# Both MLPs of a two-layer decoder step in two phases, with the second layer as seven block products over four groups of K tiles

## What is computed

```python
def squared_relu_mlp(xn, w1, w2):
    return jnp.square(jax.nn.relu(xn @ w1)) @ w2

for layer in range(DEPTH):
    xn = rms_norm(x, norm_mix[layer])
    ...
    x = x + y
    x = x + squared_relu_mlp(rms_norm(x, norm_mlp[layer]), mlp_w1[layer], mlp_w2[layer])
```

## Time and profile before

| | |
|---|---|
| median of three runs | 2669.82 us (2668.07 to 2671.2) |
| span of the profiled execution | 2668.4 us |
| busy: PE, VectorE (DVE), ScalarE (ACT), GpSimd (POOL) | 98%, 64%, 37%, 1% of the span |
| granted TensorE clock | 0.996 of full speed |
| MLP 0, from the first plain unit | 406.6 us to about 1136 us |
| MLP 1 | 1929.7 to 2660 us, then output tiles to the end |

### The profile page before, as it was taken

One profiled execution on the slowest core, in us unless ns is written; L12 is line 12 of the kernel. 1 busy time (PEld: TensorE's weight loads), 2 busy tenths in 40 slices (PEclk: granted clock), 3 DMA queues, 4 the chain that ended last, 5 costly groups with the idle time before them and its releaser, 6 DMA issues.

```text
span 2668.4 us, 48443 instructions
## 1 busy us (share of the span) xinstructions
PE 2628.0 (98%) x19052; PEld 2574.4 (96%) x19052; DVE 1709.1 (64%) x2622; ACT 980.5 (37%) x1555; POOL 24.9 (1%) x48
## 2 busy tenths in 40 slices
PE   8999999999999999999999999989999999999999
PEld 8999999999999999999999899978899999999999
DVE  5444447766666666754345898876686666666675
ACT  3111124323232323355245877755542222222222
POOL 0000000000000000000000100000000000000000
PEclk9999999999999999999999999989999999999999
DMA  3111111111010101125325566443311111111112
GB/s 116 47 47 39 48 49 34 54 34 61 31 63 31 63 31 63 32 82 160 114 76 152 130 162 155 99 147 131 99 42 40 55 39 55 39 55 39 55 39 82
DMA packets 208045, 193.05 MB, mean 72 GB/s; under 512 B 16208, under 2 KB 181008, under 8 KB 207938
## 3 DMA queue, kind: packets, MB, share of 16 engines
q1 hardware_dynamic: 188678, 182.50, 22.9%
q10 hardware_dynamic: 19260, 9.09, 1.2%
HBM read 160.93 MB, written 30.49 MB: 72 GB/s over the span
## 4 chain that ended last, share of the span: by engine, by line
PE 78%; DVE 3%; ACT 2%; issue 1%; ACTq 0%; DMA 0%; DVEq 0%
PE ps L760 29%; PE ps L748 23%; PE ps L533 13%; PE ps L1090 2%; PE ps L1005 1%; PE ps L940 1%; PE ps L1091 1%; PE ps L1092 1%; PE ps L1007 1%; PE ps L1296 1%; PE ps L1138 1%; PE ps L571 1%; PE ps L634 1%; PE ps L1200 0%; PE ps L1201 0%
## 5 line engine op out<-in xcount | busy, mean ns | idle before, releaser
L878 DVE TENSOR_TENSOR acc<-ps,acc 128x536 f32<-128x536 f32 x512 | 366.5, 717 | 254.8 <-PE ps L760 254.2
L760 PE MATMUL ps<-hidden_hi,w_hi 128*128 128x268 f32 x2048 | 423.4, 288 | 3.4 <-DVE hidden_lo L2509 1.7
L760 PE MATMUL ps<-hidden_hi,w_lo 128*128 128x268 f32 x2048 | 422.7, 288 | 0.0
L760 PE MATMUL ps<-hidden_lo,w_hi 128*128 128x268 f32 x2048 | 421.6, 287 | 0.0
L760 PEld LDWEIGHTS ps<-hidden_hi,w_hi 128*128 128x128 f32 x2048 | 321.2, 189 | 4.4 <-DVE hidden_lo L2509 2.1
L760 PEld LDWEIGHTS ps<-hidden_lo,w_hi 128*128 128x128 f32 x2048 | 322.4, 189 | 0.0
L760 PEld LDWEIGHTS ps<-hidden_hi,w_lo 128*128 128x128 f32 x2048 | 320.8, 189 | 0.0
L533 PE MATMUL ps<-x_hi,w_hi 128*128 128x358 f32 x1248 | 277.3, 330 | 4.3 <-DVE w_lo L517 4.3
L533 PE MATMUL ps<-x_hi,w_lo 128*128 128x358 f32 x1248 | 273.8, 327 | 0.0
L533 PE MATMUL ps<-x_lo,w_hi 128*128 128x358 f32 x1248 | 273.3, 327 | 0.0
L517 DVE TENSOR_TENSOR w_lo<-w_raw,w_hi 128x1024 fp32r<-128x1024 f32 x76 | 92.8, 1221 | 257.8 <-ACT w_hi L509 257.8
(11 more groups left out here) (340 smaller groups left out, 5130.9 us busy)
## 6 DMA issues: line engine op xcount, KB each, us to landing
w_raw<-in_mlp_w SPq DMA_DIRECT2D x68, 512.0 KB, 4.1
raw_a<-in_mlp_w SPq DMA_DIRECT2D x120, 256.0 KB, 3.0
w_raw<-in_conv_w_in SPq DMA_DIRECT2D x24, 512.0 KB, 3.7
w_raw<-in_w_kv SPq DMA_DIRECT2D x16, 512.0 KB, 4.9
w_raw<-in_w_o SPq DMA_DIRECT2D x16, 512.0 KB, 4.0
k_page<-in_cache_k SPq DMA_DIRECT2D x16, 512.0 KB, 4.8
v_page<-in_cache_v SPq DMA_DIRECT2D x16, 512.0 KB, 4.8
kh_rows<-staged_hi SPq DMA_DIRECT2D x8, 520.0 KB, 2.7
```

What stands on the lines that cost most here:

```text
L760: mm = pe.matmul(PS[:, 2 * p + g, 0:QW], w[k][:, P * m:P * m + P], x[:, k, a:a + QW], start=(k == 0 and j == 0), stop=(k == 1 and j == 2))
L878: dve.tensor_tensor(x, pair(p), x, ALU.add).then_inc(down_read, 1)
```

## The change

The MLP is cut into two phases.

Phase 1 runs the seven products of the 15 blocks back to back, without the second layer between them. The squares are no longer split; each quarter (128 x 536) is stored to DRAM (`h_rows`) by SyncE's queue (`store_hidden`). VectorE's preparation for the next block, which lay in `downs`, moves into `block`. `UB` becomes three buffers, and `u_sum` waits for the stores. The hidden tiles of the two plain units stay in SBUF.

Phase 2 first does the plain units' share (`plain_downs`, 16 results of 12 matmuls), then the other 30 K tiles in four groups (`GROUP` = 6, 8, 8, 8 tiles). In a group the second layer is a 2 x 2 block product (K halves, feature halves, token halves) by Winograd's scheme: 7 steps x 4 feature tiles x 3 or 4 K tiles x 6 matmuls, fully unrolled. For each group four hidden and four weight operands (A to D, 3 or 4 tiles wide) are loaded, each when the step that last used its place is done; four sums are made of each kind. The weights' sums and, from group 1 on, the hidden sums are on GpSimd; group 0's hidden sums are on VectorE. Each step's two operands are split in SBUF by ScalarE (`op_hi`, once the step before last is done) and VectorE (`op_lo`). `second_add` adds a result into one or two places; the sum `U` is added into three quarters of `ACC` at the end by GpSimd. `x_first` moves to GpSimd too. In MLP 1 the last two steps' results are interleaved, and `Y_WITH` and `Y_TAIL` are new.

```diff
-NB = 4 * D // FFB
-NQ = NB - 1
+NQ = 4 * D // FFB - 1
...
+PLAIN = [(m, h) for h in range(2) for m in range(KC)]
+UNIT_TILES = 2
+GROUP = [6, 8, 8, 8]
+NGR = len(GROUP)
+STEPS = 7
+NP2 = STEPS * NGR
+H_ROLE, W_ROLE = "ABFEDCG", "ABFEGCD"
+SUMS_BEFORE = {"A": 3, "B": 4, "C": 3, "D": 3, "E": 1, "F": 4, "G": 4}
+LOAD_ORDER = "ACDB"
...
+SECOND[1][4 * (NP2 - 2):] = [(NP2 - 2, 0), (NP2 - 2, 1), (NP2 - 1, 0), (NP2 - 2, 2), (NP2 - 1, 1), (NP2 - 2, 3), (NP2 - 1, 2),
+                             (NP2 - 1, 3)]
...
+Y_WITH = {N2 - 7: (0, 1), N2 - 6: (2, 3), N2 - 5: (4, 5), N2 - 4: (6, 7, 8), N2 - 2: (9, 10)}
+Y_TAIL = range(11, 18)
...
         def product(Q, n, l=0, first=False):
...
+            elif not first:
+                pe.wait_ge(m_read, NREAD * Q + (-4, -2, -1, 0)[n])
...
+        def second_product(l, i):
+
+            n, m = SECOND[l][i]
+            p, s, tiles = PAIRS2[l][i], n % STEPS, GROUP[n // STEPS] // 2
+            if m == 0:
+                pe.wait_ge(second_lo, NLO * l + 2 + 2 * n + 2)
...
+            for k in range(tiles):
+                for j, (w, x) in enumerate(((wh, hh), (wh, hl), (wl, hh))):
+                    for g in range(2):
+                        mm = pe.matmul(PS[:, 2 * p + g, 0:QW], w[:, k, P * m:P * m + P], x[:, k, QW * g:QW * g + QW],
+                                       start=(k == 0 and j == 0), stop=(k == tiles - 1 and j == 2))
...
+        def op_hi(l, n, to, raw):
+
+            if n > 1:
+                act.wait_ge(down_done, steps_done(l, n - 2))
+            act.activation(h_flat(to, n), h_flat(raw, n), ACT.Copy).then_inc(second_hi, 1)
...
+        def hidden_op_lo(l, n):
+
+            g, role = n // STEPS, H_ROLE[n % STEPS]
+            dve.wait_ge(second_hi, NHI * l + 4 + 2 * n + 2)
+            dve.wait_ge(h_sum, hidden_sums(l, g, SUMS_BEFORE[role]))
+            op_lo(n, h_op(n), HS[H_SLOT[g][role]])
...
+        def second_add(l, i):
...
+            targets = ((u, c11), (c11,), (u,), (c12, c22), (c12,), (c21, c22), (c21,))[n % STEPS]
...
+        def mlp_pool(l):
+
+            pool.wait_ge(unit_done, U_F[l])
+            pool.wait_ge(unit_read, U_F[l])
+            for k in range(KC // 2):
+                pool.tensor_tensor(XOF[1][:, k], half(ACC[:, k], 1), half(ACC[:, k], 0), ALU.subtract).then_inc(w_sum, 1)
+            pool.wait_ge(m_done, NPROD * NQ * (l + 1))
+            for x in range(1, 5):
+                weight_sum(l, 0, x)
+            for g in range(1, NGR):
+                for x in range(1, 5):
+                    hidden_sum(pool, l, g, x)
+                    weight_sum(l, g, x)
+            for x, (m0, h) in enumerate(((KC // 2, 0), (KC // 2, 1), (0, 1))):
+                pool.wait_ge(down_read, second_at(l, NP2 - 5 + x, 3))
+                to = ACC[:, m0:m0 + KC // 2, HALF * h:HALF * h + HALF]
+                pool.tensor_tensor(to, to, U[:, :, :], ALU.add).then_inc(w_sum, 1)
...
             def mlp(l):
...
                 with sp.Fori(1, NQ) as b:
...
+                    sp.wait_ge(m_done, NPROD * b + (NPROD * NQ * l - 4))
+                    load_a(w1, NQ * l + b, b + 1, 0)
+                    sp.wait_ge(a_lo, NPROD * b + (NPROD * NQ * l - 1))
+                    load_a(w1, NQ * l + b, b + 1, 1)
+                    for q in range(4):
+                        store_hidden(l, b, q)
...
+                for g in range(1, NGR):
+                    for s, role in enumerate(LOAD_ORDER):
+                        sp.wait_ge(down_done, steps_done(l, STEPS * (g - 1) + s))
+                        load_hidden_op(l, g, role)
+                        load_weight_op(l, g, role)
...
+            def block(Q, last=None, first=False):
+                if not first:
+                    a_sums(Q, 4)
+                    a_cut(Q, 2)
+                    a_cut(Q, 3)
                 a_cut(Q, 4)
                 u_sum(Q, 1)
                 relu_scaled(Q, 0)
-                b_cut(B, 0)
                 a_cut(Q, 5)
                 u_sum(Q, 2)
-                b_cut(B, 1)
-                hidden_lo(Q, 0)
+                if last is not None:
+                    plain_hidden_lo(last)
                 a_cut(Q, 6)
...
+                for i in range(len(PLAIN)):
+                    plain_add(l, i)
+                    if i in (6, 8, 10):
+                        if i == 6:
+                            dve.wait_ge(m_read, NREAD * NQ * (l + 1))
+                            dve.wait_ge(h_out[2], 16 * NQ * (l + 1))
+                        hidden_sum(dve, l, 0, i // 2 - 2)
+                    if i == 11:
+                        weight_op_lo(l, 0)
+                    if i == 12:
+                        hidden_op_lo(l, 0)
+                    if i == 14:
+                        hidden_sum(dve, l, 0, 4)
+                for i in range(N2):
+                    n, m = SECOND[l][i]
+                    if m == 0 and n < NP2 - 1:
+                        hidden_op_lo(l, n + 1)
+                    second_add(l, i)
+                    if m == 0 and n < NP2 - 1:
+                        weight_op_lo(l, n + 1)
```

More of the change, by code:

```diff
@@ new lines, with role_slots @@
+SUMS_BEFORE = {"A": 3, "B": 4, "C": 3, "D": 3, "E": 1, "F": 4, "G": 4}
+MADE_BY = {"E": 1, "C": 2, "F": 3, "G": 4}
+LOAD_ORDER = "ACDB"
+def role_slots(first, moves):
+    out = [first]
+    for _ in range(NGR - 1):
+        out.append({role: out[-1][old] for role, old in moves.items()})
+    return out
+H_SLOT = role_slots({"A": 0, "B": 1, "C": 2, "D": 4, "G": 5, "F": 3, "E": 9, "X": 7}, H_FROM)
+H_HI = (6, 8)
+W_SLOT = role_slots({"A": 2, "C": 3, "D": 4, "B": 5, "G": 8, "F": 9, "E": 10, "X": 6}, W_FROM)
@@ L751, in product @@
             mm.then_inc(m_done, 1)
[L753 to L766, removed]
@@ L785, in downs_first @@
[L785 to L803, removed]
@@ L805, in downs_last @@
[L805 to L813, removed]
-                p = pairs[i]
-                before = [x for x in range(i) if pairs[x] == p]
-                if before:
-                    pe.wait_ge(down_read, 2 * KC * B + before[-1] + 1)
-                elif i >= 2:
-                    pe.wait_ge(m_read, NREAD * Q + 4 + p)
-                if i >= 2:
-                    hidden_ready(Q, h, 0)
-                    down_part(m, h, p, 0)
-                hidden_ready(Q, h, 1)
-                down_part(m, h, p, 1).then_inc(down_done, 1)
-                then(i)
+        X_SUMS = (1, 3, 4, 5)
@@ L2553, in mlp @@
                     dve.memset(R[:, TOK:T], 1.0).then_inc(t_ssq, 1)
-                for k in range(4):
-                    x_first(l, k)
+                else:
+                    dve.wait_ge(conv_stored, 32)
                 for k in range(4):
@@ L2585, in mlp @@
-                x_sum_lo(l, 3, 5, 3)
-                block(Q0, B0 + 1)
-                with dve.Fori(Q0 + 1, Q0 + NQ - 1) as Q:
-                    block(Q, Q + l + 1)
-                block(Q0 + NQ - 1, B0 + NB - 1, True)
+                a_sums(Q0, 3)
+                a_sums(Q0, 4)
+                a_cut(Q0, 2)
+                a_cut(Q0, 3)
+                for k in range(4):
+                    x_sum_lo(l, 3, 5, k)
+                dve.wait_ge(second_hi, NHI * l + 2)
+                block(Q0, first=True)
```

544 lines of the change are left out of this document (345 added, 199 removed).

## The result

The changed kernel takes 2675.55 us (median of 20 runs, 2667.97 to 2682.92), the kernel before 2669.04 beside it. The ratio is 1.0019, 95% interval 1.0012 to 1.0026: slower by about a fifth of a per cent, where 0.8% faster was forecast (2649). The matmuls are gone as counted, and all that they were worth is lost again, and a little more.

The account below looks back on a forecast made before the run. PE was taken to bound both MLPs, with a matmul in flight 98% of the time. 2669.8 - 89.2 - 3.3 + 62.7 + 5.2 + 4.6 - 0.6 = 2649 us; 8-in-10 range 2580 to 2682.

Parts of the forecast that it names:

- Matmuls, -89.2: Both MLPs: 360 fewer matmuls in each, 720 at 0.1239 us, saving 89.2 us.
- phase 1 too tight: Phase 1 blocks: 1.2 us slack missed; 2 us per block adds 56 us; chance 0.09 together with an unseen wait.
- Exclusion both ways: Phase 2: GpSimd sums and VectorE two-input SBUF instructions each keep the other out; 2649 us, chance 0.58.
- rival of one way: Phase 2: GpSimd never holds VectorE up, only GpSimd waits; 2580 us, chance 0.28.
- Stalls of phase 2, +62.7: Phase 2, both MLPs: PE waits for cuts held up by GpSimd sums, 31.4 us per MLP, 62.7 in all.
- The layout: Phase 2 step timetable with sums at 4.5 and 4.3 us: PE loses 16.4 us in group 0, 7.5 in later preparing groups.
- Start, costed at nothing: MLP start: activation sums lose cover, but GpSimd's x_first and the new order bring the last some 5 us early; nothing.
- Between the phases, +5.2: Phase 1 to 2: VectorE's first cuts end at 26.4 us, due 23.8, behind GpSimd's weight sums; 2.6 us per MLP.
- End, +4.6: End of MLP 1: the last step's first result comes third in the interleave, but its cuts end at 11.6; 4.6 us lost.
- The -0.6 behind the last product: End of span: 7 tiles left after the last product, before 8, at 0.6 us each; 0.6 us saved.
- - 3.3: Second layer (L760): PE's waits from the split of hidden tiles disappear with that split, saving 3.3 us.
- longer sums: Phase 2 GpSimd sums: break-even at 4.8 us each, slower than noise from 4.9, 2680 us at 5.0; chance 0.11.

Follow-up runs that it names:

- the split version: Against the spaced, gated kernel (GpSimd hidden sums, VectorE weight sums, ScalarE order mended), only the wait before each GpSimd hidden sum removed: 2634.65 us, ratio 0.9865.
- the kernel with 308 filled: Changed kernel plus 308 extra 128-column matmuls per MLP on PE ahead of its phase 2 waits for cuts: 2687.41 us, ratio 1.0069.

## Why the prediction was wrong

- **Matmuls, -89.2: right.** 18332, and phase 1 takes 313.0 us for its 15 blocks, 20.9 each, PE full. No wait for a load or a cut anywhere in it: the rival "phase 1 too tight" is out.
- **Exclusion both ways: right in kind.** The forecast took the direction that no row showed. Its rival of one way (2580) is what the kernel would do if GpSimd only wrote (2592.7).
- **Stalls of phase 2, +62.7: 48.8 measured** (53.3 less the 4.5 at the end; 25.1 in MLP 0, 23.7 in MLP 1), although the sums were longer than priced, 4.60 and 4.85 us alone for 4.3 and 4.5. (GPSIMD Engine Reference, Elementwise in the Trainium skill has 4497 ns for 2048 columns; the trace's 4.60 us agrees.) By the forecast's own rule, 7.5 us per MLP for each 0.2 us of a sum, those prices would have given some 44 us per MLP, and a total near 2674. That number would have been right for a wrong reason: there were fewer collisions than laid out, and the rest was the clock. The layout had fourteen waits in each MLP, nearly one a step from the start of step 3 on. In MLP 0 PE had ten, at the starts of steps 3 and 5 and of the next group (in group 0 also of step 6), and one more of 0.54 us in the last group, where none was forecast.
- **The step that failed: a stall was priced at its length.** Every term of the sum is idle time; none has what PE's clock does after it. Phase 2 of MLP 0 lost 14.3 us that way. In MLP 1 the first 26 steps take 325.9 us; less 23.8 of waits and 2328 matmuls at 0.1239 that is 13.7, and the 24 matmuls behind the last wait lose 2.3 more. Together 30.3 us, unpriced. The earlier trace rows showed the clock at 1.00 with PE full; the forecast never asked what happens when PE is not.
- **Start, costed at nothing: 5.4 us late in MLP 0, 3.7 in MLP 1.** The forecast followed the product's operand, which was early indeed, and not the RMS rows, which every instruction moved ahead of them delays. GpSimd's four sums stretch VectorE's operations beside them (2.28 us for 1.34), the inverse comes 3.5 us later behind `x_fourth`, and ScalarE's copies stand behind S1's rounding. The experiments showed the last one to be enough by itself to keep the delay. Here too the stall is not the whole price: PE's waits from 415 us to the first product are 3.5 us where they were 1.4, so 2.1 of the 5.4 are waits and the other 3.3 are slow matmuls, at a granted clock of 0.83 from 420 to 440 us, 1.00 before.
- **Between the phases, +5.2: 7.8** (3.2 + 4.6 us of waits, both MLPs).
- **End, +4.6: 4.54, a right number by luck.** The prediction reckoned it from the order of roundings and cuts, and held that the three final sums of `U` fit. One of them is what held a cut up: the last step's hidden cut took 5.17 us in place of 2.39 beside it. With that addition on VectorE the wait was 2.98. The -0.6 behind the last product came to -0.1 (8.2 us from its end to the end of the span, 8.3 before).

Put together: 2669.8 - 89.2 - 3.3 + 48.8 + 7.8 + 4.5 - 0.1 + 30.3 + 5.4 + 3.7 = 2678, measured 2675.6; the terms are read from one execution of each kernel, and the sum is good to a few us. The two terms that the forecast had at nothing are 39 us, and the stalls, 14 us shorter than forecast, hid a third of that. By the forecast's own limits the result, a ratio of 1.0019, lies within 0.2% of no change, which had a chance of 0.12; slower had 0.20, of which 0.11 went to longer sums. Together 0.32 was little for a forecast gain of 0.8% in which 73 us of stalls stood against 89 us of matmuls.

## What to carry to other kernels

Work handed to GpSimd is free here only where it does not read SBUF while VectorE has an instruction with two SBUF inputs. Where the order can be chosen, one wait ahead of each GpSimd instruction puts it beside VectorE's reads of PSUM. Here that wait was worth 28.8 us, and without it the split version (2634.65) was slower than the one with all these sums on VectorE (2617.64). Price a stall on a full TensorE above its length: here 25.1 us of waits brought 14.3 us of slower matmuls, 1.3 to 2.8 us behind each wait of 1.96 us or more. When a step is moved ahead of others in a queue, ask for every consumer of what it is moved past, not only for its own.

## What the runs showed of the hardware that was not expected

- With eleven waits of 0.5 to 4.5 us in 351.6 us TensorE's granted clock was down for part of the time behind them (0.93 in the worst stretch), and what that cost did not grow with the length of the wait; after one of 1.73 and one of 3.40 us it was 0.50 for five us.
- A VectorE cut and a GpSimd sum, both reading SBUF with two inputs, run one after the other whichever starts first (6.29 us for a cut of 2.28, 5.73 us for a sum of 4.85). Beside GpSimd's fills the cut kept its 2.28 us, and beside VectorE's additions from PSUM the sum kept its 4.85.
- A matmul of 128 columns in this format costs nearly as much as one of 268: 60 of them took 6.92 us at full clock, 0.115 each, against 0.124. Had the price gone by the columns, the filling would have cost half of what it did. Whether the columns or the weight load that each has sets the 0.115, no run tells. The row is of the kernel with 308 filled:

```profile
829.96 6.92 PE L838 MATMUL ps<-ident 128*128 128x128 f32 x60
```
